# Router logits taken from the sums ahead of the second norm, and the norm's gain and bias applied behind the gather

## The reference, cut to what matters

```python
x = layer_norm(ALPHA * x + h, ln2_g[l], ln2_b[l])         # (x - mean) * rstd * g + b, per token
scores = sigmoid(x @ router_w)                            # (256, 16), router_w (1024, 16) for both layers
sel = scores + router_b
# top group of four experts by the sum of its two best sel, then the two best experts in that group
gates = (the two scores, divided by their sum)
out = sum over e of gates[:, e] * (silu(x @ w_gate[e]) * (x @ w_up[e])) @ w_down[e]
x = layer_norm(ALPHA * x + out, ln3_g[l], ln3_b[l])
```

## Time and profile before

| what | value |
|---|---|
| median of 3 runs | 738.32 us (737.9 to 740.27) |
| the profiled execution, its own time | 740.17 us |
| its span | 738.3 us |
| TensorE busy | 710.1 us (96%) |
| VectorE busy | 402.4 us (54%) |
| ScalarE busy | 270.7 us (37%) |
| GpSimd busy | 47.2 us (6%) |
| mean granted clock of TensorE | 0.983 of full speed |

### The profile page before, as it was taken

How to read it: one execution, slowest core, us unless ns; L and a number is a source line. 1 busy time by engine, 2 the same in 40 slices (tenths; PEclk the granted TensorE clock), 3 DMA queues, 4 the chain that set the end, 5 groups by cost and what they waited for, 6 DMA issues and landing times.

```text
span 738.3 us, 12040 instructions
## 1 busy us (share of the span) xinstructions
PE 710.1 (96%) x4824; PEld 572.9 (78%) x4824; DVE 402.4 (54%) x701; ACT 270.7 (37%) x465; POOL 47.2 (6%) x87
## 2 busy tenths in 40 slices
PE   6999999999999999999799999999999999999992
PEld 6998897889988875655499798888898897655541
DVE  4785887664466722111558678848646575212125
ACT  4344743355542221111333466434555131311121
POOL 2600000010001400000020000001000000000000
PEclk8999999999999999999999999999999999999996
DMA  8992334574337799999974413455633494999961
GB/s 284 341 297 86 115 115 171 173 234 163 115 127 293 270 365 394 416 417 414 355 264 158 148 58 115 152 174 187 228 115 115 172 395 196 358 421 417 418 243 60
DMA packets 62495, 176.10 MB, mean 239 GB/s; under 512 B 3824, under 2 KB 37024, under 8 KB 53216
## 3 DMA queue, kind: packets, MB, share of 16 engines
q1 hardware_dynamic: 57536, 161.75, 59.3%
q0 software_dynamic: 4032, 12.24, 5.0%
q10 hardware_dynamic: 864, 1.25, 0.6%
HBM read 174.18 MB, written 1.05 MB: 237 GB/s over the span
## 4 chain that ended last, share of the span: by engine, by line
PE 90%; DVE 5%; issue 2%; DVEq 1%; ACT 0%; POOL 0%; POOLq 0%; ACTq 0%
PE ring L2005 15%; PE ring L1589 8%; PE ring L1590 8%; PE ring L1591 8%; PE ring L2040 8%; PE quad L1589 7%; PE quad L1590 6%; PE quad L1591 6%; PE quad L2052 4%; PE ring L1631 3%; PE ring L1869 2%; PE ring L1836 2%; PE quad L1930 2%; PE ring L1738 1%; PE ring L1660 1%
## 5 line engine op out<-in xcount | busy, mean ns | idle before, releaser
L958 DVE TENSOR_TENSOR w_lo<-raw,w_hi 128x1024 fp32r<-128x1024 f32 x108 | 128.2, 1226 | 42.0 <-ACT w_hi L653 36.9
L653 ACT CAST w_hi<-raw 128x1024 fp32r<-128x1024 f32 x108 | 107.9, 1049 | 68.8 <-PE quad L1591 60.2
L1589 PE MATMUL ring<-x_hi,w_hi 128*128 128x256 f32 x352 | 104.0, 295 | 5.0 <-issue 3.6
L1590 PE MATMUL ring<-x_lo,w_hi 128*128 128x256 f32 x352 | 101.4, 288 | 0.0
L1591 PE MATMUL ring<-x_hi,w_lo 128*128 128x256 f32 x352 | 101.3, 288 | 0.0
L1589 PEld LDWEIGHTS ring<-x_hi,w_hi 128*128 128x128 f32 x352 | 69.4, 197 | 6.8 <-issue 5.7
L1590 PEld LDWEIGHTS ring<-x_lo,w_hi 128*128 128x128 f32 x352 | 69.3, 197 | 0.7 <-issue 0.5
L1591 PEld LDWEIGHTS ring<-x_hi,w_lo 128*128 128x128 f32 x352 | 69.4, 197 | 0.0
L676 ACT ACTIVATE arena<-ring 128x512 f32<-128x512 f32 (+1 forms) x66 | 35.5, 573 | 82.0 <-PE ring L1591 74.8
L1507 DVE TENSOR_TENSOR y_lo<-ring,y_hi 128x512 fp32r<-128x512 f32 x32 | 22.1, 691 | 72.9 <-ACT y_hi L912 72.9
L2005 PE MATMUL ring<-raw,x_slots 128*64 128x256 f32 x448 | 51.3, 380 | 0.0
(11 more groups left out here) (302 smaller groups left out, 1364.9 us busy)
## 6 DMA issues: line engine op xcount, KB each, us to landing
raw<-in_moe_w_gate SPq DMA_DIRECT2D x20, 1024.0 KB, 7.1
raw<-in_moe_w_up SPq DMA_DIRECT2D x16, 1024.0 KB, 7.8
w_raw<-in_moe_w_up SPq DMA_DIRECT2D x16, 1024.0 KB, 10.3
w_raw<-in_moe_w_down SPq DMA_DIRECT2D x16, 1024.0 KB, 11.4
raw<-in_w_in SPq DMA_DIRECT2D x14, 1024.0 KB, 12.1
raw<-in_moe_w_down SPq DMA_DIRECT2D x12, 1024.0 KB, 10.4
raw<-in_w_out SPq DMA_DIRECT2D x10, 1024.0 KB, 4.9
raw<-in_xattn_wk SPq DMA_DIRECT2D x8, 1024.0 KB, 5.8
```

Of the source, the lines that this page charges most:

```text
L653: nc.scalar.copy(unit_slot(u, 0, n)[:, s], raw[:, SLOT[u], s]).then_inc(hi_done, 1)
L958: low = nc.vector.tensor_tensor(unit_slot(u, 1, n)[:, s], raw[:, SLOT[u], s], unit_slot(u, 0, n)[:, s].bitcast(F32), ALU.subtract)
L1589: mm(out, a_hi, b_hi, start=first, stop=False)
L1590: mm(out, a_hi, b_lo, start=False, stop=False)
```

## The change

1. The second norm no longer ends in two passes over x before the router. Both tiles are transposed as the raw sums s = ALPHA * x + h. With g and b the gain and bias and W the router's matrix, the logits are rstd * (s @ (g W)) + (-mean * rstd) * sum(g W) + sum(b W). The 2 x 128 columns of g W and b W are made on VectorE ahead of the norm, their sums over the partitions by one product with ones, and three more small VectorE operations put the logits together. One exp serves both tiles.
2. GpSimd makes `shift` = -mean * rstd beside rstd, behind a drain. ScalarE makes z = s * rstd + shift (`normal`), and the gather's rows are split from z. The copies out of PSUM behind the gather apply gain and bias by column (`ln2_cols`).
3. TensorE's order is: 16 transposes, `logits(0)`, `logits(1)`, then 29 counts of `keep_busy`. The fillers between transposes and logits (14 counts) are gone.
4. The residual x is made later (`second_affine`: four passes of 1024 columns on VectorE) in the first pair of experts, from gain and bias loaded into `ln2_w` behind the second norm. The third norm's gain and bias are loaded earlier. Two small loads of the columns are added at the start.

```diff
-    jobs += [("xc0", "act"), ("xc1", "act"), ("rt0", "act"), ("xc2", "act"), ("xc3", "dve"), ("rt1", "act")]
+    jobs += [(f"xc{i}", "act") for i in range(4)] + [("rt0", "dve"), ("rt1", "dve")]
...
+                pool.dma_start(ln2_cols[:, 0], ln2_g.rearrange("l (p c) -> p l c", c=DC)).then_inc(const_full, 16)
+                pool.dma_start(ln2_cols[:, 1], ln2_b.rearrange("l (p c) -> p l c", c=DC)).then_inc(const_full, 16)
...
                         nc.gpsimd.tensor_tensor(lr[:, t:t + 1], lv[:, t:t + 1], minus_half[:, 0:1],
                                                 ALU.pow).then_inc(ln_rstd, 1)
+                        if i == 1:
+                            pool.drain()
+                            nc.gpsimd.tensor_tensor(shift[:, t:t + 1], neg_mean[:, t:t + 1], lr[:, t:t + 1],
+                                                    ALU.mult).then_inc(shift_ready, 1)
...
-                load_ln(ln2_g[l], ln2_b[l], 3 * l + 1)
+                load_ln(ln3_g[l], ln3_b[l], 2 * l + 1)
                 ln_power(1)
-                load_ln(ln3_g[l], ln3_b[l], 3 * l + 2)
+
+                pool.wait_ge(unit_used, used(U_O + 3, l))
+                pool.dma_start(ln2_w[0], ln2_g[l].partition_broadcast(P)).then_inc(ln2_full, 16)
+                pool.dma_start(ln2_w[1], ln2_b[l].partition_broadcast(P)).then_inc(ln2_full, 16)
...
-                turned_x(0)
-                turned_x(1)
-                act.wait_ge(unit_used, used(U_O + 3, l))
+                normal(0)
                 rows_high(0)
-                logits_exp(0)
-                turned_x(2)
+                for j in range(4):
+                    turned_x(j)
+                normal(1)
+                act.wait_ge(dve_emptied, emptied("rt1", l))
+                nc.scalar.activation(rt[:, 1], rt[:, 1], ACT.Exp, scale=-1.0).then_inc(scores_ready, 1)
                 rows_high(1)
-                logits_exp(1)
...
-                            nc.scalar.copy(x_slots[:, :, c, :],
-                                           gather_bank(0, c).rearrange("p (a b) -> p a b", a=2)).then_inc(gath_act, 1)
+                            nc.scalar.activation(x_slots[:, :, c, :], gather_bank(0, c).rearrange("p (a b) -> p a b", a=2),
+                                                 ACT.Identity, bias=ln2_cols[:, 1, l, c:c + 1],
+                                                 scale=ln2_cols[:, 0, l, c:c + 1]).then_inc(gath_act, 1)
...
+            def second_affine(l):
+
+                dve.wait_ge(ln2_full, 32 * (l + 1))
+                for t in range(T):
+                    nc.vector.scalar_tensor_tensor(X[:, t, :], X[:, t, :], mv[:, t, 0:1], ln2_w[0], ALU.subtract, ALU.mult)
+                dve.drain()
+                for t in range(T):
+                    nc.vector.scalar_tensor_tensor(X[:, t, :], X[:, t, :], lr[:, t:t + 1], ln2_w[1], ALU.mult, ALU.add)
+                dve.drain().then_inc(dense_x, 1)
...
+                for a in range(2):
+                    nc.vector.tensor_tensor(rw_parts[:, a], rw[:], view(ln2_cols[:, a, l, :], [[1, DC], [0, E]]), ALU.mult)
+                dve.drain()
+                for a in range(2):
+                    nc.vector.tensor_reduce(rt[:, 3, a, :], rw_parts[:, a].rearrange("p c e -> p e c"), AX_X, ALU.add)
+                dve.drain().then_inc(router_ready, 1)
+
+                second_sums(l, unit_used, used(U_O + 3, l))
...
+                nc.vector.tensor_copy(sel, bank("rt0")[:, E:3 * E].rearrange("p (a e) -> p a e", a=2))
+                dve.drain()
+                dve.wait_ge(shift_ready, l * T + T)
+                for t in range(T):
+                    nc.vector.scalar_tensor_tensor(rt[:, 0, t, :], sel[:, 0, :], shift[:, t:t + 1], sel[:, 1, :],
+                                                   ALU.mult, ALU.add)
+                dve.drain()
+                for t in range(T):
+                    if t:
+                        dve.wait_ge(misc_ready, misc_done("rt1", l))
+                    nc.vector.scalar_tensor_tensor(score[:, t, :], bank(f"rt{t}")[:, 0:E], lr[:, t:t + 1], rt[:, 0, t, :],
+                                                   ALU.mult, ALU.add).then_inc(dve_emptied, 1)
...
                     one_hot(1, 0)
                     one_hot(1, 1)
+                    second_affine(l)
+                    dve.sem_inc(dense_xT, 1)
...
-                transpose_x("xc", l, 2, (0,))
-                keep_busy("xc2", l, 4)
-                if l == 0:
-                    pe.wait_ge(rw_full, 16)
+                transpose_x("xc", l, 2)
+                pe.wait_ge(router_ready, l + 1)
                 pe.wait_ge(act_emptied, emptied("xc1", l))
                 logits(0)
-                keep_busy("xc2", l, 7)
-                transpose_x("xc", l, 2, (1,))
-                keep_busy("rt1", l, 3)
-                pe.wait_ge(act_emptied, emptied("xc2", l))
-                pe.wait_ge(dve_emptied, emptied("xc3", l))
+                pe.wait_ge(act_emptied, emptied("xc3", l))
                 logits(1)
 
-                keep_busy("gb1", l, 26)
+                keep_busy("gb1", l, 29)
```

More of the change, by code:

```diff
@@ L228, in hybrid_trunk_kernel @@
         minus_mean = sb("minus_mean", [P, 1])
+        neg_mean = sb("neg_mean", [P, T])
+        shift = sb("shift", [P, T])
+        ln2_cols = sb("ln2_cols", [P, 2, DEPTH, DC])
         about_mean = sb("about_mean", [P, 1])
@@ L301, in hybrid_trunk_kernel @@
         rt = at(5632, 7, T * E).rearrange("p a (t e) -> p a t e", t=T)
+        rw_parts = at(4352, 2, DC * E).rearrange("p a (c e) -> p a c e", c=DC)
         precede = at(4352, 8, PER_GROUP * PER_GROUP)
         precede2 = at(4480, 8, PER_GROUP * PER_GROUP)
-        xn_hi = rounded("xn_hi", 0, T, DC, P)
-        xn_lo = rounded("xn_lo", 2048, T, DC, P)
+        xn_hi = rounded("xn_hi", 2048, T, DC, P)
+        xn_lo = rounded("xn_lo", 0, T, DC, P)
+        z = at(6144, T, D)
+        ln2_w = [nc.alloc_sbuf_tensor_at(f"ln2_w{i}", [P, D], F32, offset=Y_HI + 4 * YC * SEQ * i)[:] for i in range(2)]
         s_t = at(4096, 2, FF)
@@ L385, in hybrid_trunk_kernel @@
         ln_read = sem("ln_read")
+        ln2_full = sem("ln2_full")
+        shift_ready = sem("shift_ready")
+        router_ready = sem("router_ready")
+        scores_ready = sem("scores_ready")
+        dense_x = sem("dense_x")
+        dense_turned = sem("dense_turned")
+        dense_xT = sem("dense_xT")
         ln_var = sem("ln_var")
@@ L558, in _ @@
             pool.dma_start(rb[:], router_b.partition_broadcast(P)).then_inc(const_full, 16)
+            with nc.allow_non_contiguous_dma(reason="a norm's gain and bias by column"):
+                pool.dma_start(ln2_cols[:, 0], ln2_g.rearrange("l (p c) -> p l c", c=DC)).then_inc(const_full, 16)
+                pool.dma_start(ln2_cols[:, 1], ln2_b.rearrange("l (p c) -> p l c", c=DC)).then_inc(const_full, 16)
             def load_small(l):
@@ L897, in late_move @@
                             act.wait_ge(gathered, l * 16 + (8 + 4 * r + c + 1))
-                            nc.scalar.copy(late_rows(r)[:, c, :], gather_bank(1, c)).then_inc(gath_act, 1)
+                            k = 4 * r + c
+                            nc.scalar.activation(late_rows(r)[:, c, :], gather_bank(1, c), ACT.Identity,
+                                                 bias=ln2_cols[:, 1, l, k:k + 1],
+                                                 scale=ln2_cols[:, 0, l, k:k + 1]).then_inc(gath_act, 1)
                     def slots_tanh(j):
@@ L1075, in first_norm, with second_sums @@
                 norm_affine(0, l, 1)
-            def second_norm(l, done, count):
+            def second_sums(l, done, count):
                 dve.wait_ge(quad_ready, l * 3 + 2)
                 norm_added(0)
-                norm_stats(0)
-                dve.wait_ge(ln_full, l * 96 + 64)
-                norm_affine(1, l, 0)
+                dve.sem_inc(x_ready, 1)
+                for a in range(2):
+                    norm_part(0, a)
+                norm_var(0, negated=True)
                 dve.wait_ge(half_ready, l + 1)
@@ L1562, in _ @@
                     dve.sem_inc(slots_ready, 2)
+                    second_affine(l)
+                    dve.wait_ge(dense_turned, l + 1)
+                    for j in range(4):
+                        t, c = j // 2, 4 * (j % 2)
+                        nc.vector.tensor_copy(xT[:, c:c + 4, t * P:(t + 1) * P],
+                                              quad[:, j, :].rearrange("p (a b) -> p a b", a=4))
+                    dve.drain().then_inc(dense_xT, 1)
                     dve.wait_ge(act_emptied, emptied("gb7", l))
@@ L2123, in moe_down @@
                         r.then_inc(unit_used, 1)
+                    pe.wait_ge(dense_x, l + 1)
+                    for t in range(T):
+                        for c in range(DC):
+                            src = X[:, t, :].rearrange("p (q c) -> p c q", c=DC)[:, c, :]
+                            o = quad[:, 2 * t + c // 4, P * (c % 4):P * (c % 4 + 1)]
```

(4 more changed lines are left out.)

61 lines of the change are left out of this document (36 added, 25 removed).

## The result

The changed kernel took 733.0 us (median of 6 runs, 730.85 to 735.07) and the kernel before, beside it, 738.1 us: a ratio of 0.9928, 95% interval 0.9904 to 0.9951. In a second comparison it was 733.3 us against 738.6, 0.9934 (0.9912 to 0.9956). So it is some 5.2 us faster, where 2.0 us were forecast. The profiled execution took 732.98 us, 731.2 us of it span: 7.1 us less span than the profiled execution of before.

The account below looks back on a forecast made before the run. The prediction took TensorE, with 90% of the chain, as the bound, its fillers setting the router's end. Two layers at 1.24 us less 0.5 us for start loads gave 2.0 us off 738.32, so 736.3 us; range 732.8 to 739.6.

Parts of the forecast that it names:

- Removed time, 2.9 us per layer at full clock: Router: with the norm's last passes gone, the counts could start at 604.35 instead of 607.25, 2.9 us earlier per layer.
- Order on TensorE: Router: transposes, product with ones and both tiles' logits in a row end at 597.78 instead of 601.36, 3.58 us earlier.
- The clock falls once in each layer: Router: 34 narrow instructions drop TensorE's clock for 3.4 us, losing 1.66 us, net gain 1.24 us per layer; chance 0.45.
- the rival of two periods: Router: clock down 6.8 us if it falls with logits left, layer 0.4 us slower than before; chance 0.25.
- Ranking ready ahead of the fillers: Router: VectorE's ranking ends at 603.2, the fillers cover it by 1.1 us and stay the bound.
- GpSimd's shift: Ahead of the transposes' copies: 0.49 us gap behind the drain, free of cost; with 2.04, TensorE waits 0.9 us.
- Identity without a table load: ScalarE: the identity function costs nothing; a table load of 1.28 us would cost 0.4 us in all.
- Copies with gain and bias: Copies from PSUM behind the gather: within 0.1 us of those without constants, bound 0.1 us each, all covered.
- The late residual in the hole: VectorE among the experts: 5.2 us in a hole of 4.53; 1.4 us of cover remain, so no cost.
- Start loads, 0.5 us: Program start: two added loads of 256 small pieces cost between nothing and 2.6 us, taken as 0.5 us.
- Sum. 2 x 1.24 - 0.5 = 2.0 us less: Whole kernel: net gain of 1.24 us in each of two layers, less 0.5 us for the start loads.
- the clock stays up: Rival, router: no clock fall, 5.3 us less, 733.0 us; up in one layer only, 734.7; chance 0.20 for both cases.

Follow-up runs that it names:

- after_arena: The changed kernel with its three small tensors behind the large block of on-chip memory instead of ahead of it: 734.5 us, ratio 0.9953.
- after_again: The changed kernel measured once more with nothing altered: 733.31 us, ratio 0.9934.
- rows_late: The changed kernel with VectorE's subtraction of tile 0's rows moved from ahead of the score operations to behind the membership: 735.21 us, ratio 0.9951.
- after_pad238: The changed kernel with 238 TensorE instructions added in layer 0's second branch, which is never run: 734.73 us, ratio 0.9945.
- affine_twice: The changed kernel with four more VectorE passes of 1024 columns ahead of the late residual's four: 747.01 us, ratio 1.0121.
- fewer20_pad: The changed kernel with 20 counts of fillers behind the logits instead of 29, and 18 never-run TensorE instructions in layer 0's second branch: 730.62 us, ratio 0.9899.
- mid17: The changed kernel with 17 counts of fillers instead of 29, 24 unrun instructions, and tile 0's subtraction moved behind tile 1's shift: 729.99 us, ratio 0.988.

## Why the prediction came out as it did

It said 736.3 and the kernel took 733.0 to 733.3. The move was 5.2 us, not 2.0. The mechanism was right and sized well where I had looked; what failed was the sum around it.

- **Removed time, 2.9 us per layer at full clock: right.** 21.36 - 18.38 = 2.98 us, from after_arena's layer 0.
- **Order on TensorE: right.** The logits end 5.44 us behind the start of the add (592.40 - 586.96), where the forecast has 597.78 - 592.17 = 5.61. Tile 0's eight transposes run beside the add, as I had assumed. Before it was 9.19 us: 3.75 us earlier, 3.58 forecast.
- **The clock falls once in each layer: right in the first profile, 3.4 us each, net 1.46 us per layer where I had 1.24.** A fall costs 19.90 - 18.38 = 1.52 us, against the 1.66 of the forecast. But it isn't once each time: in five more profiles with the row of 34 and 58 fillers (after_again, after_arena, rows_late, after_pad238, affine_twice) layer 0 had it down for 6.8, 0, 6.8, 6.8 and 6.8 us and layer 1 for 3.4, 6.8, 3.4, 3.4 and 3.4. At 6.8 us the stretch takes 21.56 us, 0.2 more than before; I had said 0.4 more. In these five stretches of twelve the rival of two periods held, and as it said, the fall had come while logits were left. I had given it 0.25.
- **Ranking ready ahead of the fillers: right.** 5.87 us behind the logits (598.27 - 592.40) where I had 5.42. With the clock down the fillers had 2.2 us too many, and 18 could go (fewer20_pad).
- **GpSimd's shift.** The gap behind the drain was 0.17 to 0.34 us, under both ends. What I had no term for was that the power itself would take 2.2 us beside VectorE's subtraction. It made z of tile 1 late on ScalarE (2.23 us of wait) but stayed under the fillers' cover.
- **Identity without a table load: right.** The function runs at 583.23 and 591.79, exp at 592.94, with no load between. (The Trainium skill, "ScalarE: Activation LUTs", section "Table sets: the hidden batching unit", says so, and the trace agrees.)
- **Copies with gain and bias: dearer than my bound of 0.1 us each.** Four on VectorE take 2.97 us instead of 2.48 and on ScalarE 2.79 instead of 2.06, and ScalarE's late ones 0.78 us each instead of 0.59. All of it lay in slack.
- **The late residual in the hole: right.** 4.96 us of passes, TensorE's L2060 without a wait, and 5.36 - 4.51 = 0.9 us of cover left by the doubled run, where I had 1.4.
- **Start loads, 0.5 us: wrong, nothing seen.** TensorE's first product of layer 0 starts at 15.17 us in the first profile after and at 14.78 to 15.23 in five more with the two loads, at 15.28 before and at 14.94 to 15.41 in three more without them.
- **The term that was missing: about 1.2 us** from the place of the block. The change adds three small tensors ahead of `arena`; I costed their loads and not what they move. 384 products got 3 to 4 ns shorter each. The chain's third such group starts 33.77 us behind the transposes before and 33.15 after, 0.62 us per layer. Of the kernel before, then of after:

```profile
523.84 1.79 PE ring L1650 x16
...
557.61 1.73 PE ring L1836 x8
```
```profile
519.32 1.79 PE ring L1723 x16
...
552.47 1.73 PE ring L1909 x8
```

- **The tail,** from the last layer's first expert product to the end, was 124.77 us before and 124.34 to 124.43 after; with the block moved alone 124.65. So 0.3 us more are gained there, with a cause that I did not look for.

The sum at full clock is then 2 x 2.98 + 1.2 + 0.3 = 7.5 us. Against this stands the clock: over 14 executions of the changed kernel its mean was 0.981, over the 21 of the one before in the second comparison 0.986. That is 2 x (0.019 x 732 - 0.014 x 737) = 7.2 us more at the lower level, a little over two falls of 3.4 us; at 1.52 us each they cost 3.2 us. 4.3 us remain, and 5.2 were measured, with an interval of about 1.6 us on either side. What lies between is not settled.

The step that failed is "Sum. 2 x 1.24 - 0.5 = 2.0 us less": its router part measured 2 x 1.46 in the profile, the start's 0.5 was not there, and the 1.5 us of place and tail stood in it at nothing: 2.9 + 1.5 = 4.4 us. The largest part of the miss is the place of the block, which the prediction left out without a reason. Of the 5.2 us measured, 0.8 us stay without a cause. The rival "the clock stays up", at 733.0, hit the number and is wrong all the same: the clock fell in both layers of the profile. The signs that I had named came out on every point: clock 0.50 behind the logits in both layers, L1992 (L1922 before) at the end of the fillers, no gap ahead of L2060. (The two profiled spans differ by 7.1 us, more than 5.2; 3.1 of it lie ahead of layer 0's router, where the profile of before had the clock down for 10.2 us and that of after for 3.4.)

## What to carry to other kernels

Cost what an edit moves in memory and in the instruction stream, not only what it runs: a few small tensors ahead of a large block were worth 1.2 us in this kernel's traces, and 18 instructions fewer ahead of a jump cost 2.8 us. When a stretch is shortened at its head, count its covering work anew: with 34 fillers instead of 58, near what the ranking needs, one subtraction moved and unrun instructions to keep the code in place, the same change gave 8.4 us (mid17) instead of 5.2. Fillers pay for the clock only where they cost no time; here, between narrow instructions whose result is waited for, they cost as much as they saved or more.

## What the hardware showed that I had not expected

- TensorE, busy without a pause in 34 narrow instructions and the fillers behind, had its clock fall from 2.4 to 1.2 GHz in eleven of the twelve stretches of six profiles, for 3.4 or 6.8 us, and in one not at all, with the same instructions. Broken up by 10 or 6 fillers on either side of `logits(0)`, the row brought no fall in four stretches, though in two of them the clock fell behind the counts. (The Trainium skill, "TensorE: Matmul & The Clock Gate", section "What's actually happening", lets the clock follow how busy the array has been recently. The traces agree only in part: the clock fell while the profile shows TensorE busy without a pause.)
- A GpSimd operation on 128x1 took 2.19 us instead of 0.54 beside a two-input VectorE pass of 1024 columns, and ended 0.4 us behind it.
- The same matmul of 256 columns took 288 or 285 ns, and one of 512 columns 397 or 389, by the place of an operand's block in on-chip memory; moves of 160, 192 and 224 bytes had different effects, and the rule stays open.
- With 18 TensorE instructions fewer ahead of a jump, a pause of 2.30 us stood four instructions behind it; with 18 that never run added, it was gone.
